# A top-k that strikes out the 16 lowest of 128 scores, and causal products grouped behind three tiles' products

## The chip, the core and the metric

The kernel runs on one core of one Trainium2 chip. The metric is the device time of one execution in microseconds (us). The core has five instruction queues that run side by side and meet only at semaphores: TensorE (PE, matrix products; its weight loads are listed apart as PEld), VectorE (DVE), ScalarE (ACT), GpSimd (POOL) and SyncE (SP, which issues DMAs). Products land in PSUM, where VectorE and ScalarE fetch them; everything else lies in SBUF.

## The reference

One decoder layer of 512 tokens (plus 16 meta tokens in front, 528 keys in all) with two attention branches, cut to what matters here:

```python
# branch A: an indexer scores every key, the best `topk` = 128 are attended to
rel = einsum('bqhd,bkd->bqhk', qi, ki) * scale_i
idx_score = einsum('bqhk,bqh->bqk', relu(rel), wi)
idx_score = where(s_pos < N_META, inf, idx_score)      # the 16 meta tokens are always picked
idx_score = where(causal, idx_score, -inf)
_, sel = lax.top_k(idx_score, topk)                    # so 112 of the others
valid = sel <= t_pos
la = einsum('bqhd,bqkhd->bqhk', qa, k_sel) * scale_a + bias
pa = softmax(where(valid, la, NEG))
# branch B: latent attention over all keys, 8 heads
lb = (q_nope @ k_nope + q_pe @ k_pe) * scale_b
lb = where(causal, lb, NEG)
pb = softmax(lb)
# then
mixed = concat([oa * silu(ga), ob * silu(gb)])
out = layer_norm(ALPHA * h + mixed @ w_out)
```

## The kernel before, in words

The 512 query rows are four tiles of 128 (`QT`). Tile i sees the 16 meta keys and 128(i+1) further ones, so `NK` is 144, 272, 400 and 528 columns. The indexer's scores of all tiles lie in `iw` with 128, 256, 384 and 512 columns.

**Order of the work.** `schedule()` writes one list, `ORDER`, by hand, and each engine walks it and takes its part of each entry. A projection job (`J`) is a group of products into one of two alternating banks of `ps_j`; ScalarE, VectorE or both read it out, and TensorE may start the job after the next only when this bank is free (line 1194 is the product of nearly all jobs). The jobs named below: `qn` and `kn` make queries and keys of two heads of branch B (`q_b`, `k_b`; ScalarE takes one head at lines 745 and 749, VectorE the other at lines 971 and 975), `va` makes values (`v_a`, ScalarE, line 756), `uv` the values of branch B.

**Top-k.** It needs 112 of up to 512 scores a row. One round finds the eight largest of a row (`max`, MAX8, line 1037) and overwrites them in place with `TAKEN` (`match_replace`, line 1041, with a short load of the eight values ahead). 14 rounds (`ROUNDS`) are made on each tile. Each round has two halves (`TOPK_HALF`): a long one with tile 3 (512 columns) and a short one with tiles 0, 1 and 2. `pick(n)` puts the next n half rounds into the order, 28 in all: 7 in two groups between the last projection jobs ahead of branch B, 3 ahead of its first values, the rest between the heads. Behind the last, `MASK` (line 1047) makes from `iw` a mask that is 2^100 where a score was not taken; branch A's heads need it.

**Heads.** Entries `S`, `X`, `R`, `TP` and `PV` with g = 0 to 15 are the heads: 0 to 7 of branch B, 8 to 15 of branch A. `S` is the scores in `ps_s`: TensorE, in two units, tiles 3, 1 and 0 first and then tile 2 (`UNITS`), and row minima on VectorE (`mn`, line 1069; signs are turned, so minima stand for maxima). `X` is the exponential on ScalarE (`pr`, line 835), `R` the reciprocal on VectorE (line 1083) and the scaling on GpSimd (line 648), `TP` transposes (line 1404 on), `PV` the product with the values. TensorE's `S` of a head waits until ScalarE has read the scores of the head before.

**Causal products.** For heads 0 to 7 the last 144 columns of each tile's scores get 2^100 added where a key lies in the future. It is a product too, of a bf16 identity with the bf16 table `causal` (line 1389), accumulated into the same columns behind the tile's fp32 product (line 1385; each appears as two instructions, tile 3 in two pieces of 240 and 288 columns).

Of the kernel before, what the change touches and what calls it, by code (L numbers as in the profile page):

```python
# [25 lines left out]
P = 128  # L26
# [87 lines left out]
def schedule():  # L114
# [42 lines left out]
    def pick(count):  # L157

        for _ in range(min(count, len(halves))):
            order.append(("TOPK", *halves.pop(0)))  # L160

    for h in range(HEADS):
# [11 lines left out]
        if h in (3, 4):  # L174
            order.append(("CAST", h - 3))
    job("qpe", 1)
    pick(2)
    job("gate", 6, extra=0)
    pick(5)
    job("uv", 0, 0, extra=0)  # L180
    job("uv", 0, 1, extra=0)
    need(BLOCKS[0], 2)
# [13 lines left out]
    for g in range(2 * HEADS):  # L196
        p = (g % HEADS) // 2
        more = p + 1 < PAIRS

        if g < HEADS:  # L200
            jobs = [("va", *va.pop(0)) for _ in range((1, 1, 2, 0, 2, 1, 2, 0)[g])]
            if g % 2 and more:
                jobs = [("qn", p + 1)] + jobs + [("kn", p + 1, 0), ("kn", p + 1, 1)]
            if g == HEADS - 1:
                jobs = [("qa", 0), ("ka", 0, 0), ("ka", 0, 1)]
        elif more:
            jobs = [("ka", p + 1, 0), ("ka", p + 1, 1)] if g % 2 else [("qa", p + 1)]
        else:
            jobs = [("out", *outs.pop(0)) for _ in range(6 if g % 2 == 0 else 4)]
        pair = (g - 3) // 2 if g >= 3 and g % 2 else None  # L210
        late = pair is not None and g >= HEADS - 1 and more or g == HEADS - 1
        order.append(("S", g))
        if g > HEADS and g % 2 and more:
            job(*jobs.pop(0), extra=0)
        order.append(("X", g))
        if g < HEADS:
            pick(1)
        if jobs[0][0] == "qn":
            order.append(("QPE", jobs[0][1]))
            job(*jobs.pop(0), extra=0)  # L220
            order[-2:] = order[:-3:-1]
        if pair is not None and not late:
            order += [("PV", pair, 0), ("PV", pair, 1)]
        if g >= HEADS and not more:
            for _ in range(3 if g % 2 == 0 else 2):
                job(*jobs.pop(0))
        order.append(("R", g))
        if HEADS <= g < 2 * HEADS - 2:
            order.append(("FOLD", g - HEADS + 2))
        if g < HEADS and g % 2 == 0:  # L230
            pick(1 if g == 0 else 2)
        if g == HEADS - 1:
            assert not halves
            order += [("MASK",), ("BIAS",), ("FOLD", 0), ("FOLD", 1)]
        for n, j in enumerate(jobs):
            if late and n == len(jobs) - 1:
                order.append(("PV", pair, 0))
            job(*j, extra=int(j[0] == "out"))
        if g < HEADS - 1 and g % 2:
            pick(1)  # L240
        if g:
            order += [("TP", g - 1), ("J", "tq", g - 1, 0)]
        if late:
            order.append(("PV", pair, 1))
        need(BLOCKS[0], 2)
        if HEADS + 1 <= g < HEADS + 5:
            order.append(("MIX", 4 + g - HEADS - 1))
        if g == 2 * HEADS - 2:
            order += [("MIX", 0), ("MIX", 1)]
# [36 lines left out]
MIXED = [s[1] for s in ORDER if s[0] == "MIX"]  # L286
LAST_JOB = [NJ[last_reader(_b)] for _b in range(len(BLOCKS))]
LAST_IN_JOB = max(n for n, j in enumerate(JOBS) if j[0] not in ("out", "tq"))
TOPK_HALF = [(3,), (0, 1, 2)]


def build(nc, x, meta, ln_emb_g, ln_emb_b, rel_bias, ln_post_g, ln_post_b, weights, gains, onehot, cos_t,
# [6 lines left out]
    with ctx:  # L299
# [26 lines left out]
        identb = sb("identb", [P, P], BF16)  # L326
        causal = sb("causal", [P, 144], BF16)
        wi = sb("wi", [P, QT, HEADS])
        top8 = sb("top8", [P, QT, 8])
        st = sb("st", [P, 5, 2, 6])  # L330
        st4 = sb("st4", [P, 4, 6])
# [45 lines left out]
        post_g, post_b = pr[:, 0, 0:D], pr[:, 1, 0:D]  # L377
        oh_sb = iw[0:BUCKETS, 0:VECW]
        vec_sb = mix[0:HEADS, 0:2, :].rearrange("p a n -> p (a n)")[:, 0:VECW]

        ps_s = ctx.enter_context(nc.psum_tensor("ps_s", [P, 1536], F32))
        ps_t = ctx.enter_context(nc.psum_tensor("ps_t", [P, 1024], F32))
# [68 lines left out]
        bn_s = sem("bn_s")  # L451
        eps = sem("eps")
        kp = sem("kp")
        squared = sem("squared")
        rope_m = sem("rope_m")

# [409 lines left out]
        def _(dve):  # L866
# [51 lines left out]
            for stage, *arg in ORDER:  # L918
# [76 lines left out]
                elif stage == "SWAP":  # L995
                    dve.wait_ge(job_act, BY_ACT[NJ["kk", 0, 1] + 1])
                    dve.stream_shuffle(k_b[HD:HD + ROPE, 0, :], k_b[HD:HD + ROPE, 1, :], SWAP).then_inc(kp, 1)
                elif stage == "NORM":
                    n = arg[0]
                    dve.wait_ge(root, (6, 8)[n])  # L1000
# [27 lines left out]
                elif stage == "TOPK":  # L1028

                    r, half = arg  # L1030
                    tiles, done = TOPK_HALF[half], topk[half]
                    if r == 0:
                        dve.wait_ge(i_add, 4 * HEADS)
                    for n, i in enumerate(tiles):
                        if r:
                            dve.wait_ge(done, len(tiles) * (2 * r - 1) + n + 1)
                        dve.max(top8[:, i, :], iw[:, IOFF[i]:IOFF[i] + P * (i + 1)]).then_inc(done, 1)  # L1037
                    for n, i in enumerate(tiles):
                        a = iw[:, IOFF[i]:IOFF[i] + P * (i + 1)]
                        dve.wait_ge(done, len(tiles) * 2 * r + n + 1)  # L1040
                        dve.match_replace(out=a, in_to_replace=top8[:, i, :], in_values=a,  # L1041
                                          imm_value=TAKEN).then_inc(done, 1)
                elif stage == "MASK":
                    for half in range(2):
                        dve.wait_ge(topk[half], 2 * len(TOPK_HALF[half]) * ROUNDS)
                    for i in range(QT):
                        dve.tensor_scalar(mask[:, POFF[i] + META:POFF[i] + NK[i]],
                                          iw[:, IOFF[i]:IOFF[i] + P * (i + 1)], TAKEN, MASKED, ALU.is_gt,
                                          ALU.mult).then_inc(masked, 1)
                    dve.wait_ge(masked, QT)  # L1050

                    dve.tensor_tensor(mask[:, 0:144], mask[:, 0:144], causal[:, :], ALU.add).then_inc(masked, 1)
# [104 lines left out]
        def _(pe):  # L1157
# [59 lines left out]
            for stage, *arg in ORDER:  # L1217
# [140 lines left out]
                elif stage == "S":  # L1358
# [14 lines left out]
                    for u, tiles in enumerate(UNITS):  # L1373
# [6 lines left out]
                        for i in tiles:  # L1380
                            for a, b in ([(0, 240), (240, 528)] if i == 3 else [(0, NK[i])]):
                                dst = ps_s[:, SOFF[i] + a:SOFF[i] + b]
                                if g < HEADS:
                                    c0 = NK[i] - 144
                                    pe.matmul(dst, q_b[:, e, i * P:(i + 1) * P], k_b[:, e, a:b], start=True,  # L1385
                                              stop=b <= c0)
                                    if b > c0:
                                        lo = max(a, c0)
                                        last = pe.matmul(ps_s[:, SOFF[i] + lo:SOFF[i] + b], identb[:, :],
                                                         causal[:, lo - c0:b - c0], start=False, stop=True)  # L1390
                                else:
                                    for v in range(2):
                                        last = pe.matmul(dst, qs[:, p % 2, e, i * P:(i + 1) * P], ks[:, e, v, a:b],  # L1393
                                                         start=v == 0, stop=v == 1)
                        last.then_inc(s_mm, 1)
                elif stage == "TP":

# [113 lines left out]
```

## Time and profile before

| | |
|---|---|
| median of three runs | 356.42 us (355.7 to 357.35) |
| the profiled execution | 356.88 us, span of its instructions 355.1 us |
| TensorE busy, mean granted clock | 329.3 us (93%), 0.992 |
| VectorE busy | 233.6 us (66%) |
| ScalarE busy | 171.5 us (48%) |
| GpSimd busy | 188.0 us (53%) |

A span is the time from the first instruction to the last. The profile's views used below: a page with shares and groups; the chain of work that ended last, followed back from the last instruction; a list of who waited for whom; groups of instructions by shape; and a timeline, where neighbours of one kind are merged and the time idle ahead of them stands in brackets. Records of one engine may overlap by the part of an instruction that is pipelined, so the chain's pieces, which don't overlap, give what each adds.

### The profile page before, as it was taken

The page shows a single profiled execution, that of the slowest core. Times are in us where ns is not written, and L with a number is a line of the kernel's source. Part 1 is how long each engine was busy: PE and PEld are TensorE (multiplying, and loading weights), DVE is VectorE, ACT ScalarE, POOL GpSimd, SP SyncE. Part 2 cuts the span into 40 slices and gives each one's busy share as a digit, 9 for nine tenths or more (in the row PEclk, how much of TensorE's full clock was granted, in tenths as well). Part 3 has the DMA queues.
Part 4 walks back from the last instruction along what each step waited for, and adds up shares of the span by engine and source line. Part 5 has one row for each costly group of instructions (what it writes and reads, how often), then busy time and mean ns, then how long its engine had stood idle before and what let it go on. Part 6 is the DMA issues. An engine that isn't in the chain of part 4 may idle for free.

```text
span 355.1 us, 6148 instructions
## 1 busy us (share of the span) xinstructions
PE 329.3 (93%) x2147; PEld 272.4 (77%) x2147; DVE 233.6 (66%) x618; ACT 171.5 (48%) x378; POOL 188.0 (53%) x172
## 2 busy tenths in 40 slices
PE   1799999999999979999999999999898999999991
PEld 1488887878778758886878887887776897897980
DVE  6762210289865999897985875557787866434666
ACT  4674543352463435556543553763775653612230
POOL 4432999777240442455313495876765581640564
PEclk9999999999999999999999999999999999999996
DMA  7463333249311131112200150431212110140023
GB/s 278 154 212 142 122 116 115 90 122 304 116 59 59 61 119 34 57 59 71 68 7 9 59 210 3 137 101 50 81 56 90 60 53 10 59 121 0 2 118 118
DMA packets 11565, 32.86 MB, mean 93 GB/s; under 512 B 2392, under 2 KB 2392, under 8 KB 11536
## 3 DMA queue, kind: packets, MB, share of 16 engines
q1 hardware_dynamic: 8944, 27.08, 22.4%
q10 hardware_dynamic: 2592, 5.40, 5.1%
q8 instruction: 17, 0.28, 0.3%
q14 instruction: 12, 0.10, 0.1%
HBM read 29.83 MB, written 4.81 MB: 98 GB/s over the span
## 4 chain that ended last, share of the span: by engine, by line
PE 72%; DVE 14%; issue 6%; ACT 6%; DMA 2%; SPq 0%; DVEq 0%; ACTq 0%
PE ps_j L1194 46%; PE ps_s L1385 5%; PE ps_o L1434 5%; PE ps_j L1236 2%; DVE iw L1041 2%; PE ps_t L1404 2%; ACT pr L835 2%; DMA res<-in_x 2%; PE ps_s L1355 2%; DVE top L1037 2%; DVE iw L1025 1%; PE ps_t L1409 1%; PE ps_s L1393 1%; DVE pr L1071 1%; PE ps_j L1247 1%
## 5 line engine op out<-in xcount | busy, mean ns | idle before, releaser
L518 POOL TENSOR_TENSOR wl<-raw,wh 128x1024 fp32r<-128x1024 f32 (+2 forms) x33 | 77.3, 2350 | 73.7 <-ACT wh L525 73.6
L1194 PE MATMUL ps_j<-hh,wh 128*128 128x512 f32 (+2 forms) x224 | 79.3, 354 | 2.4 <-DVE qs L950 1.4
L1194 PE MATMUL ps_j<-hl,wh 128*128 128x512 f32 (+2 forms) x224 | 77.9, 348 | 0.0
L1194 PE MATMUL ps_j<-hh,wl 128*128 128x512 f32 (+2 forms) x224 | 77.6, 347 | 0.0
L648 POOL TENSOR_SCALAR pr<-pr,rden 128x528 f32<-128x528 f32 (+1 forms) x64 | 34.2, 553 | 45.2 <-DVE rden L1083 45.2
L1194 PEld LDWEIGHTS ps_j<-hh,wh 128*128 128x128 f32 (+1 forms) x224 | 41.8, 186 | 13.1 <-issue 7.3
L1194 PEld LDWEIGHTS ps_j<-hh,wl 128*128 128x128 f32 (+1 forms) x224 | 41.8, 187 | 5.5
L1194 PEld LDWEIGHTS ps_j<-hl,wh 128*128 128x128 f32 (+1 forms) x224 | 41.8, 186 | 5.5 <-issue 0.2
L525 ACT ACTIVATE wh<-raw 128x1024 fp32r<-128x1024 f32 (+2 forms) x35 | 35.9, 1040 | 2.7 <-DMA raw<-in_weights 2.7
L1194 PE MATMUL ps_j<-wh,hh 128*128 128x256 f32 (+1 forms) x112 | 32.1, 287 | 1.0 <-DVE res L994 1.0
L1194 PE MATMUL ps_j<-wl,hh 128*128 128x256 f32 (+1 forms) x112 | 31.4, 281 | 0.0
L1194 PE MATMUL ps_j<-wh,hl 128*128 128x256 f32 (+1 forms) x112 | 31.4, 280 | 0.0
L658 POOL TENSOR_TENSOR bm<-bias,mask 128x144 f32<-128x144 f32 (+3 forms) x32 | 27.4, 888 | 0.0
L1041 DVE MATCH_REPLACE8 iw<-top,iw 128x512 f32<-128x512 f32 (+3 forms) x56 | 26.2, 475 | 0.0
L1037 DVE MAX8 top<-iw 128x8 f32<-128x512 f32 (+3 forms) x56 | 24.5, 478 | 0.0
L835 ACT ACTIVATE pr<-pr,mn 128x528 f32<-128x528 f32 (+3 forms) x32 | 18.0, 566 | 13.2 <-DVE mn L1071 13.1
L835 ACT ACTIVATE pr<-ps_s,mn 128x528 f32<-128x528 f32 (+3 forms) x32 | 16.9, 540 | 15.0 <-DVE mn L1069 15.0
L1385 PE MATMUL ps_s<-k_b,q_b 96*128 96x240 f32 (+4 forms) x80 | 22.3, 406 | 0.0
L1194 PEld LDWEIGHTS ps_j<-wh,hh 128*128 128x128 f32 (+1 forms) x112 | 19.6, 175 | 3.3 <-issue 2.9
L738 ACT ACTIVATE mix<-ps_j 128x512 f32<-128x512 f32 x8 | 4.8, 598 | 33.7 <-PE ps_j L1194 33.7
L1194 PEld LDWEIGHTS ps_j<-wh,hl 128*128 128x128 f32 (+1 forms) x112 | 19.6, 175 | 0.4
L1194 PEld LDWEIGHTS ps_j<-wl,hh 128*128 128x128 f32 (+1 forms) x112 | 19.6, 175 | 0.3
(224 smaller groups left out, 754.7 us busy)
## 6 DMA issues: line engine op xcount, KB each, us to landing
raw<-in_weights SPq DMA_DIRECT2D x37, 512.0 KB, 3.5
bias_by_distance<-bias_vector ACTq DMA_DIRECT2D x1, 2624.0 KB, 13.8
bias<-bias_by_distance ACTq DMA_DIRECT2D x8, 264.0 KB, 3.7
res<-in_x SPq DMA_DIRECT2D x4, 512.0 KB, 4.9
out<-res SPq DMA_DIRECT2D x3, 512.0 KB, 2.6
pt<-in_ln_emb_g SPq DMA_DIRECT2D x1, 512.0 KB, 5.5
pt<-in_ln_emb_b SPq DMA_DIRECT2D x1, 512.0 KB, 6.9
q_b<-qpe ACTq DMA_DIRECT2D x8, 64.0 KB, 2.0
```

The source lines that it names most:

```text
L518: eng.tensor_tensor(ring_of(False, b), raw_of(b), ring_of(True, b).bitcast(F32), ALU.subtract).then_inc(done, 1)
L525: act.activation(ring_of(True, b), raw_of(b), ACT.Copy).then_inc(w_high, 1)
L648: pool.tensor_scalar(a, a, rden[:, k, n:n + 1], 1.0, ALU.mult, ALU.mult).then_inc(scaled, 1)
L658: pool.tensor_tensor(bm[:, h % 2, s], bias[:, h % 4, T - NK[i]:T], mask[:, s], ALU.add).then_inc(folded, 1)
L835: act.activation(dst, src, ACT.Exp, bias=mn[:, k, n:n + 1], scale=-1.0, accum_out=den[:, k, n:n + 1]).then_inc(e_done, 1)
L1037: dve.max(top8[:, i, :], iw[:, IOFF[i]:IOFF[i] + P * (i + 1)]).then_inc(done, 1)
L1041: dve.match_replace(out=a, in_to_replace=top8[:, i, :], in_values=a, imm_value=TAKEN).then_inc(done, 1)
L1194: last = pe.matmul(dst, a, b, start=n == 0 and part[0], stop=n == count - 1 and part[1])
L1236: last = pe.transpose(bank[:, i * P:(i + 1) * P], pr[:, n % 2, a:a + P], ident[:, :])
L1355: last = pe.matmul(ibank(e, u)[:, a:a + w], qs[r, (h // 2) % 2, q, i * P:(i + 1) * P], ki[r, k, META:META + w], start=n == 0, stop=n == 2)
L1385: pe.matmul(dst, q_b[:, e, i * P:(i + 1) * P], k_b[:, e, a:b], start=True, stop=b <= c0)
L1434: last = pe.matmul(ps_o[HD * e:HD * e + HD, q0:NQ], v[0:r, j, c:c + HD], pt[0:r, e, CO[j]:CO[j] + NQ - q0], start=j == 0, stop=j == 4)
```

## The change

Two things are changed, and `pick` counts with them.

*Tile 0's top-k.* Of its 128 scores 112 are to be taken, so 16 are left. A new entry `FLIP` copies the 128 columns of tile 0 times -1 into a new tile `drop`, in reversed order of columns (`drop_back` is `drop` read or written backwards). Two rounds of MAX8 and match-and-replace on `drop` (`DROP_ROUNDS` = (128 - 112) / 8 = 2) mark the 16 lowest. The short half has three tiles in rounds 0 and 1 and two tiles, 1 and 2, in rounds 2 to 13. `MASK` reads tile 0's part from `drop_back` with the comparison the other way round. `topk_count` replaces the products that counted signals.

*Picks.* The second of the two groups ahead of branch B has 4 halves where it had 5; behind head 0 there are 2 where there was 1.

*Causal products.* They no longer stand behind each tile's product but in a loop behind the products of all tiles of the unit: three in succession in the first unit, one in the second. Tile 3's is one product of 144 columns, as before. The products of tiles 1 and 0 no longer start an accumulation of their own (`start=i >= 2`); tile 3's products, ahead of them in the same banks, do.

```diff
     job("qpe", 1)
+    order.append(("FLIP",))
     pick(2)
     job("gate", 6, extra=0)
-    pick(5)
+    pick(4)
...
         if g < HEADS and g % 2 == 0:
-            pick(1 if g == 0 else 2)
+            pick(2)
...
-TOPK_HALF = [(3,), (0, 1, 2)]
+DROP_ROUNDS = (P - PICKED) // 8
+TOPK_HALF = [lambda r: (3,), lambda r: (0, 1, 2) if r < DROP_ROUNDS else (1, 2)]
+
+
+def topk_count(r, half):
+
+    return 2 * sum(len(TOPK_HALF[half](n)) for n in range(r))
...
+        drop = sb("drop", [P, P])
...
+        drop_back = bass.AP(drop[:, :].tensor, drop[:, :].offset + P - 1, [drop[:, :].ap[0], [-1, P]])
...
+                elif stage == "FLIP":
+                    dve.wait_ge(i_add, 4 * HEADS)
+                    dve.tensor_scalar(drop_back, iw[:, IOFF[0]:IOFF[0] + P], -1.0, None, ALU.mult).then_inc(flipped, 1)
...
                     r, half = arg
-                    tiles, done = TOPK_HALF[half], topk[half]
+                    tiles, done = TOPK_HALF[half](r), topk[half]
                     if r == 0:
                         dve.wait_ge(i_add, 4 * HEADS)
+                        dve.wait_ge(flipped, 1)
                     for n, i in enumerate(tiles):
+                        a = iw[:, IOFF[i]:IOFF[i] + P * (i + 1)] if i else drop[:, :]
...
-                                          iw[:, IOFF[i]:IOFF[i] + P * (i + 1)], TAKEN, MASKED, ALU.is_gt,
-                                          ALU.mult).then_inc(masked, 1)
+                                          iw[:, IOFF[i]:IOFF[i] + P * (i + 1)] if i else drop_back, TAKEN, MASKED,
+                                          ALU.is_gt if i else ALU.is_le, ALU.mult).then_inc(masked, 1)
...
                                 if g < HEADS:
-                                    c0 = NK[i] - 144
-                                    pe.matmul(dst, q_b[:, e, i * P:(i + 1) * P], k_b[:, e, a:b], start=True,
-                                              stop=b <= c0)
-                                    if b > c0:
-                                        lo = max(a, c0)
-                                        last = pe.matmul(ps_s[:, SOFF[i] + lo:SOFF[i] + b], identb[:, :],
-                                                         causal[:, lo - c0:b - c0], start=False, stop=True)
+                                    pe.matmul(dst, q_b[:, e, i * P:(i + 1) * P], k_b[:, e, a:b], start=i >= 2,
+                                              stop=b <= NK[i] - 144, skip_group_check=True)
...
+                        if g < HEADS:
+                            for i in tiles:
+                                a = SOFF[i] + NK[i] - 144
+                                last = pe.matmul(ps_s[:, a:a + 144], identb[:, :], causal[:, :], start=False, stop=True,
+                                                 skip_group_check=True)
```

How the instructions stand now. First VectorE's queue ahead of its copy of the first `q_b`. Before (`top` is the eight values found, `iw` the scores; the last row belongs to the job `kn`):

```order
L1037 MAX top<-iw 128x8
L1041 MATCH_REPLACE iw<-top,iw 128x512
L1037 MAX top<-iw 128x8 x3
L1041 MATCH_REPLACE iw<-top,iw 128x128
L1041 MATCH_REPLACE iw<-top,iw 128x256
L1041 MATCH_REPLACE iw<-top,iw 128x384
L1037 MAX top<-iw 128x8
L1041 MATCH_REPLACE iw<-top,iw 128x512
L971 TENSOR_SCALAR q_b<-ps_j 64x512
L975 COPY k_b<-ps_j 64x264 x2
```

The same place in the changed kernel, whose line numbers are 11 to 17 higher:

```order
L1054 MAX top<-iw 128x8
L1058 MATCH_REPLACE iw<-top,iw 128x512
L1054 MAX top<-iw 128x8 x2
L1058 MATCH_REPLACE iw<-top,iw 128x256
L1058 MATCH_REPLACE iw<-top,iw 128x384
L982 TENSOR_SCALAR q_b<-ps_j 64x512
L986 COPY k_b<-ps_j 64x264 x2
```

The last long half has moved behind `q_b` and `k_b`, and the short half of round 2 has two tiles.

Second, VectorE between the row minima (`mn`) of head 0 and those of head 1. Before:

```order
L1069 TENSOR_REDUCE mn<-ps_s 128x1 x4
L1037 MAX top<-iw 128x8
L1041 MATCH_REPLACE iw<-top,iw 128x512
L1083 RECIPROCAL rden<-den 128x3
L1083 RECIPROCAL rden<-den 128x1
L1037 MAX top<-iw 128x8 x3
L1041 MATCH_REPLACE iw<-top,iw 128x128
L1041 MATCH_REPLACE iw<-top,iw 128x256
L1041 MATCH_REPLACE iw<-top,iw 128x384
L1069 TENSOR_REDUCE mn<-ps_s 128x1 x4
```

Changed:

```order
L1086 TENSOR_REDUCE mn<-ps_s 128x1 x4
L1054 MAX top<-iw 128x8 x2
L1058 MATCH_REPLACE iw<-top,iw 128x256
L1058 MATCH_REPLACE iw<-top,iw 128x384
L1100 RECIPROCAL rden<-den 128x3
L1100 RECIPROCAL rden<-den 128x1
L1054 MAX top<-iw 128x8
L1058 MATCH_REPLACE iw<-top,iw 128x512
L1054 MAX top<-iw 128x8 x2
L1058 MATCH_REPLACE iw<-top,iw 128x256
L1058 MATCH_REPLACE iw<-top,iw 128x384
L1086 TENSOR_REDUCE mn<-ps_s 128x1 x4
```

Two halves, one long and one short, have become three: short, long, short.

Third, TensorE in the scores of one head of branch B (`k_b` with `q_b` is a tile's product, `causal` with `identb` the causal one). Before:

```order
L1385 MATMUL ps_s<-k_b,q_b 128x240
L1385 MATMUL ps_s<-k_b,q_b 128x288
L1389 MATMUL ps_s<-causal,identb 128x144
L1385 MATMUL ps_s<-k_b,q_b 128x272
L1389 MATMUL ps_s<-causal,identb 128x144
L1385 MATMUL ps_s<-k_b,q_b 128x144
L1389 MATMUL ps_s<-causal,identb 128x144
L1385 MATMUL ps_s<-k_b,q_b 128x400
L1389 MATMUL ps_s<-causal,identb 128x144
```

Changed:

```order
L1401 MATMUL ps_s<-k_b,q_b 128x240
L1401 MATMUL ps_s<-k_b,q_b 128x288
L1401 MATMUL ps_s<-k_b,q_b 128x272
L1401 MATMUL ps_s<-k_b,q_b 128x144
L1410 MATMUL ps_s<-causal,identb 128x144 x3
L1401 MATMUL ps_s<-k_b,q_b 128x400
L1410 MATMUL ps_s<-causal,identb 128x144
```

The number of products is the same; the causal ones of tiles 3, 1 and 0 now follow one another.

## Rows read from the trace of the kernel before

**Rows 1.** The page, part 1: busy us, share of the span, instructions of each engine

```profile
PE 329.3 (93%) x2147; PEld 272.4 (77%) x2147; DVE 233.6 (66%) x618; ACT 171.5 (48%) x378; POOL 188.0 (53%) x172
```

**Rows 2.** The page, part 4: the chain that ended last, shares by engine

```profile
PE 72%; DVE 14%; issue 6%; ACT 6%; DMA 2%; SPq 0%; DVEq 0%; ACTq 0%
```

**Rows 3.** TensorE's waits between 105 and 206 us: us in total, times, longest

```profile
PE ps_j L1194 <- DVE q_b L971: 1.6, 1, 1.6
PE ps_j L1194 <- ACT v_a L756: 0.6, 2, 0.3
```

**Rows 4.** The chain in order of time, 119 to 136 us: start, us, what

```profile
120.59 0.97 DVE top L1037 x3
121.57 1.19 DVE iw L1041 x3
...
131.28 0.70 DVE q_b L971
...
132.12 4.35 PE ps_j L1194 x30
```

**Rows 5.** Timeline at the wait, VectorE then ScalarE: start, us, instruction [idle before]

```profile
129.78 0.68 DVE L1037 MAX8 top<-iw 128x8 f32<-128x512 f32 x1
...
130.18 0.59 ACT L745 ACTIVATE q_b<-ps_j 64x512 f32<-64x512 f32 x1 [0.80 <-PE ps_j L1194]
```

**Rows 6.** VectorE: two match loads in the timeline, then groups: busy us, mean ns

```profile
121.50 0.07 DVE L1041 MATCH_VALUE_LOAD iw<-top,iw 128x8 f32 x1
...
121.75 0.08 DVE L1041 MATCH_VALUE_LOAD iw<-top,iw 128x8 f32 x1
...
L1037 DVE MAX8 top<-iw 128x8 f32<-128x128 f32 x14 | 3.9, 281 | 0.0
...
L897 DVE TENSOR_TENSOR iw<-iw,gain 128x128 f32<-128x128 f32 x1 | 0.3, 293 | 0.0
...
L1001 DVE RECIPROCAL tmp<-tmp 128x528 f32<-128x528 f32 x1 | 3.4, 3436 | 0.0
```

**Rows 7.** The chain, transposes and scores of head 2: start, us, what

```profile
150.43 0.44 PE ps_t L1404 x4
...
151.89 0.89 PE ps_s L1385 x4
152.78 0.06 PE ps_s L1389
152.84 0.51 PE ps_s L1385 x2
...
153.41 0.29 PE ps_s L1385 x2
...
153.77 0.72 PE ps_s L1385 x2
```

**Rows 8.** TensorE's loads by shape, and line 1389's products (ns min/median/max)

```profile
L1194 PEld LDWEIGHTS ps_j<-wh,hh 128*128 128x128 f32 x96 | 18.1, 188 | 3.0 <-issue 2.9
...
L1389 PEld LDWEIGHTS ps_s<-causal,identb 128*128 128x128 bf16 x32 | 3.1, 98 | 1.9
...
L1194 PEld LDWEIGHTS ps_j<-wh,hh 128*16 128x16 f32 x16 | 1.5, 94 | 0.3
...
L1389 PE MATMUL ps_s<-causal,identb x32: 227/228/228, 137.3 to 205.3; 128*128 128x144 bf16 x32
```

**Rows 9.** Timeline of heads 0 and 1, VectorE then ScalarE

```profile
138.93 1.75 DVE L1069 TENSOR_REDUCE mn<-ps_s 128x1 f32<-128x528 f32 x4
...
144.70 1.74 DVE L1069 TENSOR_REDUCE mn<-ps_s 128x1 f32<-128x528 f32 x4
...
148.07 0.59 ACT L745 ACTIVATE q_b<-ps_j 64x512 f32<-64x512 f32 x1
...
149.18 0.38 ACT L756 ACTIVATE v_a<-ps_j 128x256 f32<-128x256 f32 x1 [0.52 <-PE ps_j L1194]
```

**Rows 10.** The chain behind head 9

```profile
242.66 0.94 ACT wh L525
```

More of the change, by code:

```diff
@@ L453, in build @@
         kp = sem("kp")
+        flipped = sem("flipped")
         squared = sem("squared")
@@ L1030, in _ @@
                     r, half = arg
-                    tiles, done = TOPK_HALF[half], topk[half]
+                    tiles, done = TOPK_HALF[half](r), topk[half]
                     if r == 0:
                         dve.wait_ge(i_add, 4 * HEADS)
+                        dve.wait_ge(flipped, 1)
                     for n, i in enumerate(tiles):
+                        a = iw[:, IOFF[i]:IOFF[i] + P * (i + 1)] if i else drop[:, :]
                         if r:
-                            dve.wait_ge(done, len(tiles) * (2 * r - 1) + n + 1)
-                        dve.max(top8[:, i, :], iw[:, IOFF[i]:IOFF[i] + P * (i + 1)]).then_inc(done, 1)
+                            last = TOPK_HALF[half](r - 1)
+                            dve.wait_ge(done, topk_count(r, half) - len(last) + last.index(i) + 1)
+                        dve.max(top8[:, i, :], a).then_inc(done, 1)
                     for n, i in enumerate(tiles):
-                        a = iw[:, IOFF[i]:IOFF[i] + P * (i + 1)]
-                        dve.wait_ge(done, len(tiles) * 2 * r + n + 1)
+                        a = iw[:, IOFF[i]:IOFF[i] + P * (i + 1)] if i else drop[:, :]
+                        dve.wait_ge(done, topk_count(r, half) + n + 1)
                         dve.match_replace(out=a, in_to_replace=top8[:, i, :], in_values=a,
@@ L1044, in _ @@
                     for half in range(2):
-                        dve.wait_ge(topk[half], 2 * len(TOPK_HALF[half]) * ROUNDS)
+                        dve.wait_ge(topk[half], topk_count(ROUNDS, half))
                     for i in range(QT):
                         dve.tensor_scalar(mask[:, POFF[i] + META:POFF[i] + NK[i]],
-                                          iw[:, IOFF[i]:IOFF[i] + P * (i + 1)], TAKEN, MASKED, ALU.is_gt,
-                                          ALU.mult).then_inc(masked, 1)
+                                          iw[:, IOFF[i]:IOFF[i] + P * (i + 1)] if i else drop_back, TAKEN, MASKED,
+                                          ALU.is_gt if i else ALU.is_le, ALU.mult).then_inc(masked, 1)
                     dve.wait_ge(masked, QT)
```

## The prediction, made before the changed kernel was run

> **What bounds the kernel now.** I read the busy shares first: TensorE is busy for 93% of the span, VectorE for 66% [rows 1]. Busy shares do not say who waits, so I went to the chain of work that ended last: 72% of it is TensorE, 14% VectorE [rows 2]. A VectorE saving is therefore worth only what it takes out of that 14%. Third, I asked for TensorE's own waits. Between 105 and 206 us one stands out, 1.6 us on a VectorE copy out of PSUM, `q_b`; behind it come two waits on ScalarE's `v_a`, 0.6 us together [rows 3]. The chain shows what stands ahead of that copy: from 119 to 131 us it runs through nothing but top-k rounds, `top` and `iw` on VectorE, then `q_b`, and then TensorE starts again at 132.12 [rows 4]. TensorE's queue is not short of work there; VectorE's queue is long. Everywhere else in the first eight heads TensorE has to be made shorter itself, or nothing is gained.
>
> **Part 1, VectorE: the tile of 128 rows leaves twelve rounds, and one half round moves behind `q_b`.** A short half round (three tiles) costs 0.97 us of MAX8 and 1.19 us of match-and-replace, 2.16 together [rows 4]. The 128-wide tile's share: its MAX8 is recorded with 281 ns [rows 6], but records of neighbours overlap. The three operations take 0.97 us for 768 columns; by columns alone 128 of them are 0.16, and I take 0.19. Its match load starts at 121.50 and the next tile's at 121.75, so 0.25 [rows 6]. Together 0.44 us a round, 12 rounds, 5.3 us less on VectorE. Only the part ahead of `q_b` can reach TensorE: one of the three short halves there loses its tile, -0.44. The moved long half takes from 129.78 to 131.28, -1.50 [rows 5]. Added is the reversed negated copy (`FLIP`). No row has an operand that runs backwards. The nearest ordinary operation of 128x128 f32 took 0.29 us [rows 6]; the slowest rate per element on this engine, the reciprocal of 528 columns in 3.44 us, would make it 0.83 [rows 6]. I take 0.3, since it is a plain multiply. VectorE would then be ready for `q_b` at 131.28 - 1.50 - 0.44 + 0.3 = 129.6 us (130.2 at the upper bound).
>
> But the data is not there at 129.6. ScalarE reads the same PSUM bank for its half of the product, waited 0.80 us for TensorE, and started at 130.18 [rows 5]. So VectorE's copy starts at 130.18 instead of 131.28, and TensorE resumes at 131.0 instead of 132.12: **1.1 us gained**. The price of `FLIP` is hidden in the 0.6 us in which VectorE now waits; only beyond that does it count. What is late next at this place is TensorE's own previous product, and the 0.5 to 0.8 us that remain idle are one copy and its signals.
>
> The other ten rounds save nothing by themselves. They lie beside TensorE's work, and after 133 us no wait of TensorE names VectorE until past the eighth head [rows 3].
>
> **What the second half round in head 0 costs.** Between the row minima of head 0 and of head 1 there stood one long and one short half; now there are one long and two short ones of 1.7 us. Before, the minima of head 0 began at 138.93 and of head 1 at 144.70, both directly behind a top-k, with no idle time ahead [rows 9]. After: three half rounds (1.4 + 1.7 + 1.4) from 132.0 end at 136.5, TensorE's scores are ready at about 137.3, minima end at 139.0, then 1.7 + 0.2 + 1.4 + 1.7 brings the minima of head 1 to about 144.1. That is 0.6 us earlier than before while TensorE is 1.3 us earlier. ScalarE's copy of the next `q_b` followed those minima by 3.4 us (148.07) [rows 9], so it comes at 147.5 and is read out at 148.0. TensorE, which ended the product before just ahead of 149.18, where ScalarE takes `v_a` [rows 9], wants that bank at about 147.85. It waits some 0.3 us. Half of this is swallowed by the wait on `v_a` that follows, because ScalarE's queue is then no longer ahead of its data. I charge **0.15 us lost**. From head 2 on VectorE is again ahead of TensorE.
>
> **Part 2, TensorE: 16 changes of operand type fewer.** For each of the first eight heads four causal products (bf16 identity as weights) stood each between two fp32 products. The rows of one head: 528 score columns took 0.89 us, 1.69 ns a column. By that 272, 144 and 400 columns should take 0.46, 0.24 and 0.67; they took 0.51, 0.29 and 0.72 [rows 7]. So the first fp32 product behind a causal one is about 0.048 us late, and the causal one itself takes 0.06. The load rows explain it. A load of 128x16 is recorded with 94 ns and one of 128x128 with 188, thus 0.84 ns a column on some 81 ns of fixed record; the fp32 weights need about 107 ns, and a causal product of 0.06 us hides only 0.06 of that. The bf16 identity is recorded with 98 ns, so about 17 above the fixed part [rows 8]: it fits behind 0.06 us. In the new order c, c, c, product, the first two causal products of each head are followed by a causal one. Each such place costs 0.06 instead of 0.06 to 0.07 plus 0.048: 0.053 saved, two a head, eight heads: **0.85 us gained**. Bounds: if a causal behind a causal came no faster than the transposes with a 128-column identity, 0.44 us for four or 0.11 each [rows 7], against 0.115 now, the gain would be 0.1; if nothing but streaming remained, 0.9.
>
> The measured load and streaming rows speak for 0.06. The Trainium skill ("TensorE: Matmul & The Clock Gate", section "Back-to-back issue gap") speaks against it: it says that in a stream of load-and-multiply pairs both set the spacing, and gives about 81 ns a pair at 128 columns. By that figure, an estimate from the page, a pair of 144 columns would take some 0.088 us and the term would be 0.4 in place of 0.85, the whole 355.0 us. No row of this trace has two bf16 pairs in succession, so the trace does not decide it.
>
> The products of tiles 1 and 0 no longer clear their accumulators first; nothing is issued more or less for it, I take 0. The mask of tile 0 is read backwards: it costs at most what the copy may cost, and VectorE waits for ScalarE behind it.
>
> **Sum.** 1.1 + 0.85 - 0.15 = 1.8 us. Everything later hangs on TensorE: the long stall after 241 us begins with ScalarE reading what TensorE just wrote, then `wh` at 242.66 [rows 10], the weight remainder on GpSimd, the mixture's remainder and the minima on VectorE. It moves as one piece, so I see no fixed point at which the 1.8 us is given back. The profiled execution took 356.88 us (span 355.1 and 1.8 around it), 0.46 above the median. Its sum gives 355.1; from the median of 356.42 it gives **354.6 us**.
>
> **Rivals.**
> *Identity loads not hidden.* Then the causal term is 0.1 and the total is 1.1 + 0.1 - 0.15 = 1.05: 355.4 us. For it: the transposes' 0.11 each. Against: their fp32 identity is recorded with a longer load than the bf16 one. The page's figure lies between, 355.0.
> *Given back in heads 0 and 1.* VectorE's extra half round delays head 1's exponentials, `q_b` and the product behind them by the whole 1.1 us; only the causal 0.85 would stay: 355.6 us. It would need the minima of head 1 no earlier than 144.7. My walk has them at 144.1, with 0.6 us between.
> *More than forecast.* The two `v_a` waits of 0.6 us [rows 3] shrink too, since ScalarE gets its exponentials earlier: 354.0 us. Against: they wait for TensorE's own product.
> *Slower: successive causal products wait for one another.* Three now accumulate in a row into two neighbouring banks. If each had to drain before the next, the step would be the 0.228 us that a causal product's record lasts from start to end [rows 8] rather than 0.06, a loss of 0.11 at 16 places, 1.8 us, against 1.0 gained: 357.2 us. From a step of about 0.18 us it decides the sign. Against: a causal product already follows the fp32 product whose very columns it adds to, with no gap between the pieces of the chain [rows 7].
> *The change doesn't do what it says.* The identity loads are all still issued, one with each product; if their number fell, the term would be at its upper end of 0.9.
>
> **Chances.** Forecast 0.57 (its own range 354.1 to 355.1). Loads partly or wholly exposed, 355.0 to 355.4, 0.20. Given back 0.08. More than forecast 0.09. Slower 0.06. The range of 8 in 10 goes from 353.7 to 356.0. A measurement here can tell about 0.5% from no change, that is 1.8 us, or 354.64: the forecast sits on this line. From the cases: faster by over 0.5%: half of the forecast's and all of the larger gain's, less a little, 0.46. Within 0.5%: 0.50. Slower by over 0.5%: 0.04.
>
> **What would show it.** TensorE's wait for `q_b` at 130 us falls from 1.6 to about 0.5 and it resumes near 131.0; `FLIP` is 0.3 us and VectorE idles ahead of `q_b`; VectorE is 5 us less busy; the chain has three causal products in about 0.18 us and then 0.72 for 400 columns; the head's scores take 2.55 us in place of 2.66. I am wrong if TensorE resumes after 131.5, if the three causal products take over 0.25 us, if a new wait over 0.4 us stands in head 1, or if TensorE's wait ahead of head 9 grows by what was gained.

## The result and the profile after

| | before | changed |
|---|---|---|
| median of 11 runs each, on one chip | 356.18 us (354.06 to 357.69) | 353.12 us (351.73 to 353.81) |
| ratio, 95% interval | | 0.991 (0.9886 to 0.9934) |
| second comparison, beside other kernels: median | 355.39 us (28 runs) | 353.45 us (11 runs) |
| ratio, 95% interval | | 0.9944 (0.9926 to 0.9963) |
| span of the profiled execution | 355.1 us | 350.2 us |
| VectorE busy | 233.6 us | 226.2 us |

The forecast was 354.6 us, 1.8 us or 0.5% below 356.42, with a range from 353.7 to 356.0. The first comparison gives 3.1 us, and 353.12 lies below the range; the second gives 1.9 to 2.0. The sign was right, the step that each part was said to make can be found in the trace, and what is to be explained is the rest. Part of it lies in the start: the forecast went out from 356.42, the median of three runs, and the kernel before had a median of 355.39 to 355.63 in four later comparisons (11 to 28 runs each). The changed kernel's two medians, 353.12 and 353.45, lie close together.

Of VectorE's 7.4 us, 2.4 belong to one subtraction that was held up in the first trace of before (below). The other four traces of before have VectorE busy for 230.6 to 230.8 us and the changed kernel's three for 226.2 to 226.4: the change takes 4.4 us off it, where 5 were forecast.

Where TensorE waits in the changed kernel between 105 and 206 us (as in [rows 3]: us in total, times, longest):

```profile
PE ps_j L1211 <- DVE q_b L982: 0.5, 1, 0.5
PE ps_j L1211 <- ACT q_b L756: 0.4, 1, 0.4
PE ps_j L1211 <- ACT v_a L767: 0.3, 1, 0.3
```

The wait of 1.6 us on `q_b` is 0.5 now, a new one of 0.4 stands in head 1, and one of the two waits on `v_a` is gone. VectorE at the place of [rows 5 and 6], and ScalarE's half of the same copy:

```profile
118.25 0.22 DVE L1011 TENSOR_SCALAR drop<-iw 128x128 f32<-128x128 f32 x1
...
129.31 0.69 DVE L982 TENSOR_SCALAR q_b<-ps_j 64x512 f32<-64x512 f32 x1 [0.45 <-PE ps_j L1211]
...
129.31 0.59 ACT L756 ACTIVATE q_b<-ps_j 64x512 f32<-64x512 f32 x1 [0.80 <-PE ps_j L1211]
```

The reversed copy took 0.22 us, and VectorE now sits idle for 0.45 us before `q_b` and starts in the same moment as ScalarE. (Both stand 0.87 us earlier than ScalarE's row of before for a reason outside the change: TensorE's granted clock rose at 16.7 us in this execution and at 18.7 in that one. When it rises differs from one execution to the next, whatever the kernel, and is taken out of the table below.) The scores of head 2 in the chain, against [rows 7]:

```profile
149.76 1.59 PE ps_s L1401 x8
151.35 0.19 PE ps_s L1410 x3
151.54 0.72 PE ps_s L1401 x2
152.27 0.07 PE ps_s L1410
```

Three causal products take 0.19 us, 0.062 each. The whole is 2.57 us instead of 2.66.

A table by stage shows where the spans differ. It is worked out from the starts of the same products, by their count, in every trace: from TensorE's stop at the first `q_b` to the transposes behind head 1 (A), to head 7 (B), to head 11 (C), to head 13 (D), and to the last product (E), in us:

| trace | A | B | C | D | E |
|---|---|---|---|---|---|
| before | 20.59 | 65.86 | 43.71 | 29.86 | 56.69 |
| before, second trace (again_before) | 21.92 | 65.88 | 43.80 | 27.76 | 56.52 |
| before, third trace (look_before_2) | 20.57 | 65.86 | 43.78 | 27.75 | 56.48 |
| changed | 19.34 | 65.21 | 43.71 | 27.81 | 56.66 |
| changed, second trace (again_after) | 19.33 | 65.21 | 43.71 | 27.81 | 56.53 |

A and B hold what was forecast: 1.25 and 0.65, together 1.9 us. Two further things show. Stage D of the forecast's own trace is 2.1 us longer than in the four others, and stage A of the kernel before is 1.35 us longer in one of its three.

**Stage D.** VectorE's subtraction `mbl` behind head 11 in the first trace of before, and then GpSimd there:

```profile
265.47 3.33 DVE L1108 TENSOR_TENSOR mbl<-mix,mbh 128x512 fp32r<-128x512 f32 x1 [0.74 <-ACT mbh L853]
...
262.70 3.19 POOL L658 TENSOR_TENSOR bm<-bias,mask 128x144 f32<-128x144 f32 x4
265.85 2.40 POOL L518 TENSOR_TENSOR wl<-raw,wh 128x1024 fp32r<-128x1024 f32 x1
```

And the same in the changed kernel:

```profile
262.70 0.97 DVE L1125 TENSOR_TENSOR mbl<-mix,mbh 128x512 fp32r<-128x512 f32 x1 [0.74 <-ACT mbh L864]
...
259.93 3.19 POOL L669 TENSOR_TENSOR bm<-bias,mask 128x144 f32<-128x144 f32 x4
263.08 2.85 POOL L529 TENSOR_TENSOR wl<-raw,wh 128x1024 fp32r<-128x1024 f32 x1
```

In both, `mbl` is issued 0.38 us before GpSimd ends its additions `bm`. In the first GpSimd goes on with `wl` at full speed (2.40) and VectorE stands until that is over. In the second VectorE goes first and `wl` takes 2.85. The times from `bm` to `mbl` are equal to 0.01 us (2.77) in the two traces, so it was not a shift between these two engines that set the order. What hangs on it: the row minima of head 12 come 2.4 us later, and TensorE waits 1.4 us on `qs`, a row that this trace of the changed kernel doesn't have. The Trainium skill ("SBUF — State Buffer", section "SBUF: two separate sides") says that VectorE with two SBUF inputs and GpSimd share a pair of ports by an exclusive lock, and that the loser stands for a whole instruction. The trace agrees on the price (3.33 = 0.38 + 2.40 + about 0.55, which is left for the subtraction itself). The rule gives the pair to whoever starts first; here VectorE was issued first, was blocked by `bm`, and then lost to the next GpSimd instruction once and won otherwise, which the rule doesn't settle.

**Stage A.** The second trace of before. The chain from `q_b` on, and engines by stretch (PE, PEld, DVE, ACT and POOL busy, then the granted clock):

```profile
130.34 0.70 DVE q_b L971
131.04 0.14 issue
131.18 5.87 PE ps_j L1194 x30
137.05 0.89 PE ps_s L1385 x4
```
```profile
132.70:136.20 3.50, 3.50 (x19) 3.50 (x19) 3.47 (x13) 0.39 (x1) 0.00 (x0) 0.51 0.15 37
```

The 30 products that took 4.35 us in [rows 4] took 5.87. From 132.7 to 136.2 us the granted clock was 0.51, the lower of the two levels (1.2 GHz of 2.4). What TensorE did before it: it had stood for 1.6 us on `q_b` and then worked without a pause from 131.18 on.

### The profile page after: what moved, and what is told of

Same layout as the page of the kernel before. It is cut to its first block, busy times and chain, and to the rows that moved or that the text cites. A ratio compares the mean times of both kernels' runs of the same rounds, so it can differ in the third digit from the quotient of the medians.

```text
span 350.2 us, 6115 instructions
## 1 busy us (share of the span) xinstructions
PE 327.1 (93%) x2147; PEld 272.4 (78%) x2147; DVE 226.2 (65%) x583; ACT 171.4 (49%) x378; POOL 188.5 (54%) x172
## 4 chain that ended last, share of the span: by engine, by line
PE 73%; DVE 11%; issue 6%; ACT 5%; POOL 2%; DMA 2%; SPq 0%; DVEq 0%; ACTq 0%; POOLq 0%
PE ps_j L1211 47%; PE ps_o L1451 5%; PE ps_s L1401 4%; PE ps_s L1405 2%; PE ps_j L1253 2%; POOL wl L529 2%; PE ps_t L1421 2%; PE ps_s L1372 2%; DMA res<-in_x 2%; ACT pr L846 2%; PE ps_t L1426 1%; DVE iw L1039 1%; DVE tmp L1015 1%; PE ps_j L1264 1%; DVE v_b L1015 1%
## 5 line engine op out<-in xcount | busy, mean ns | idle before, releaser
L1058 DVE MATCH_REPLACE8 iw<-top,iw 128x512 f32<-128x512 f32 (+2 forms) x42 | 22.6, 543 | 0.0
L1054 DVE MAX8 top<-iw 128x8 f32<-128x512 f32 (+2 forms) x42 | 21.8, 547 | 0.1
L1401 PE MATMUL ps_s<-k_b,q_b 96*128 96x240 f32 (+4 forms) x80 | 21.2, 396 | 0.0
```

The costliest lines, as they stand in the source:

```text
L1054: dve.max(top8[:, i, :], a).then_inc(done, 1)
```

## The experiments

Two theories of stage D were set against each other. A: the order of VectorE and GpSimd behind head 11 differs from execution to execution. B: the change decides it. A third, C, came later and is about stage A: the long wait on `q_b` itself makes the clock fall in part of the executions.

### A second trace of each kernel

No edit.

> The kernel before, unchanged, for a second profile. Theory A: the subtraction mbl on VectorE behind head 11 and the weight remainder wl on GpSimd fall due within 0.4 us of each other and either may go first, by chance. Then this trace may show that subtraction either with about 3.3 us (and TensorE's waits of 1.4 us on qs and a step of some 2.0 us behind it) or with about 1.0 us and none of these. Theory B: the kernel before always loses there, and the changed one always wins because of a shift the change makes: 3.3 us here again.

> The changed kernel, unchanged, for a second profile. Theory A: its subtraction mbl behind head 11 may come out at 1.0 us or at 3.3 us. Theory B: 1.0 us again.

Measured 355.14 and 354.06 us. Both traces have the quick order:

```profile
265.99 0.92 DVE L1108 TENSOR_TENSOR mbl<-mix,mbh 128x512 fp32r<-128x512 f32 x1 [0.80 <-ACT mbh L853]
```

Theory B falls as it stands: the kernel before has the quick order too. That the change makes the slow order rarer is not excluded (see the counts below). That the clock falls in this trace was not foreseen.

### Each part alone

```diff
 causal_only: before, and
-                                    pe.matmul(dst, ..., start=True, stop=b <= c0)
-                                    if b > c0:
-                                        ...   (causal product of the tile)
+                                    pe.matmul(dst, ..., start=i >= 2, stop=b <= NK[i] - 144, ...)
+                        if g < HEADS:
+                            for i in tiles:
+                                ...           (causal products of the unit)
 topk_only: the changed kernel with this turned back
```

> The kernel before with the grouped causal products alone. By the step between two causal products of 0.062 us and the head's scores of 2.57 us after, against 2.67 before, eight heads give 0.8 us: ratio 0.9977. Theory A (the order at the end of head 11 falls by chance): 0.8 us, and on average no more. Theory B (a shift of TensorE against GpSimd makes the later gain): up to 2.8 us if this part carries the shift, ratio 0.992.

> The changed kernel with each causal product back behind its tile's product. TensorE resumes 1.1 us earlier behind the first q_b, and of this some 0.15 to 0.2 goes again in head 1: 0.9 to 1.0 us, ratio 0.9973. Theory B, if this part carries the shift: up to 3 us, ratio 0.9915.

causal_only: 354.94 against 355.4, ratio 0.9981 (0.9969 to 0.9992). Its stage B is 65.32 against 65.86. Its trace shows the fall of the clock too (0.51 from 133.5 to 137.0 us), so its stage A of 21.74 is to be held against the 21.92 of the second trace of before: 0.18 less. topk_only: 353.89, ratio 0.9953 (0.9936 to 0.9971), its stages A and B are 19.43 and 65.86. In us that is 0.7 and 1.7. The causal part is as forecast. The other gives more than its 1.16 us of stage A; its interval (1.0 to 2.3) takes in that and what the clock adds (below). Neither carries 3 us.

### The order behind head 11, forced both ways

```diff
 before_hold6: before, GpSimd ahead of the weight remainder behind head 11
+                        if arg[0] in HOLD:
+                            pool.wait_ge(mix_l, MIXED.index(HOLD[arg[0]]) + 1)
 after_lose6 (and before_lose6): VectorE ahead of the subtraction there
+                    for b in HOLD:
+                        if HOLD[b] == c and not LOW_BY_DVE[b]:
+                            low_made(dve, b)
```

> The kernel before, in which GpSimd waits, ahead of the weight remainder that it makes behind head 11, until VectorE's subtraction mbl of the same place is done. VectorE then always goes first. Theory A and B alike: mbl there takes 1.0 us, TensorE's wait of 1.4 us on qs and the step before head 13's scores go, 2.0 us less than an execution that loses. Theory A: the kernel before loses in part of its executions only, so the median falls by 1 to 2 us and its spread narrows. If the later gain has another cause, the time is that of before.

> The changed kernel, in which VectorE waits, ahead of its subtraction mbl behind head 11, until GpSimd has made its weight remainder. GpSimd always goes first. mbl ends some 2.4 us later, the row minima of head 12 too, and TensorE waits for qs again: by the sum of part 1 and part 2 the kernel is then 1.6 to 1.9 us faster than before where before loses as well, ratio about 0.995 to 0.997, instead of 0.991. If the later gain has another cause, the ratio stays at 0.991.

> The kernel before, in which VectorE's subtraction behind head 11 always waits for GpSimd's weight remainder. Theory A (order by chance, slow order rare): 2.0 us slower than before, ratio 1.0055. If before were mostly in the slow order by itself: ratio 1.001 or less.

> The kernel before, a further trace. Theory A: subtraction behind head 11 at 0.9 to 1.0 us or at 3.3 us; the granted clock falls for 3.4 us at about 133 us in one of five executions.

| kernel | median | before beside it | ratio, 95% interval | stage D |
|---|---|---|---|---|
| before_hold6 | 355.51 | 355.47 | 1.0001 (0.9985 to 1.0016) | 27.81 |
| before_lose6 | 357.77 | 355.63 | 1.0065 (1.0039 to 1.0091) | 30.06 |
| after_lose6 | 355.53 | 355.47 | 1.0001 (0.9987 to 1.0015) | 30.07 |

The slow order costs 2.1 to 2.3 us in either kernel and eats the change's whole gain. Two expectations failed here. before_hold6 gained nothing where 1 to 2 us had been expected, and after_lose6 came out level with before where a ratio of 0.995 to 0.997 had been expected, for the same reason: the kernel before is in the quick order nearly always. Two more traces (look_before_3, look_before_4) had it too. Of all 13 traces in which the order was free, one has the slow order: the one from which the forecast was made. By kind it is one of seven with the old top-k (before five times, causal_only, picks_only) and none of six with the new, too few to tell whether the change matters for it.

### The count of half rounds

```diff
 picks_only: before, with
-    pick(5)
+    pick(4)
-            pick(1 if g == 0 else 2)
+            pick(2)
 after_oldpicks: the changed kernel, with these turned back
 after_pickmoved: the changed kernel, with
-            pick(2)
+            pick({0: 1, 4: 3}.get(g, 2))
```

> The kernel before with only the count of half rounds changed (4 in the second group ahead of branch B, 2 behind head 0); tile 0 stays in all 14 rounds and the causal products stay apart. VectorE is free for q_b at 131.28 - 1.50 = 129.8, still ahead of its data at 130.18, so TensorE gains the same 1.1 us there. But the minima of head 1 come 1.3 us later than in the changed kernel (three short halves of 2.2 instead of 1.7 us), and TensorE's wait on ScalarE's q_b in head 1 grows from 0.4 to 1.5 us or more: net about 0.1 us less, ratio 0.9997, if the tile's removal is needed for the gain. Rival: the gain of 1.0 us and more stands, ratio 0.997, and the 5.3 us of VectorE's work taken away were worth nothing.

> The changed kernel with the old count of half rounds (5 and 1). VectorE comes to q_b at 131.28 - 0.44 + 0.22 = 131.1, TensorE waits 1.4 us there instead of 0.5 and gains 0.2 us only; the wait on q_b in head 1 goes. By these terms 1.0 us against before (0.8 by the causal products, 0.2 here), ratio 0.997. Theory C (a wait of 1.4 us or more at this place lets TensorE's granted clock fall for some us in part of the executions; with the wait of 0.5 us it never fell in six traces): mean clocks of 0.987 to 0.989 appear among its runs again, as in 7 of 23 runs of before, and in none of the changed kernel.

> The changed kernel with one half round behind head 0 (as before) and three behind head 4. Head 1's minima come 1.4 us earlier, ScalarE's q_b too, and TensorE's wait of 0.4 us on it goes; the wait on v_a behind it comes back, some 0.25 us: net 0.1 to 0.2 us less, which five rounds cannot tell from nothing; the trace can. Rival: three half rounds behind head 4 delay head 5's minima until TensorE waits for exponentials: up to 1 us slower.

picks_only: 355.0 against 355.39, ratio 0.9994 (0.9973 to 1.0015). Two of its waits between 105 and 206 us:

```profile
PE ps_j L1194 <- ACT v_a L756: 1.4, 2, 1.1
PE ps_j L1194 <- DVE q_b L971: 0.5, 1, 0.5
```

The wait on `q_b` falls to 0.5 by the counts alone, without tile 0's removal, and comes back as one of 1.1 us in head 1, where 1.5 or more had been expected. (The list puts it down to `v_a`, but the product starts at 149.09 us, before `v_a` ends at 149.11; it comes 0.25 us behind the end of `q_b` in ScalarE, as it does in the changed kernel.) Stage A is 20.23, only 0.36 less than before. Taking tile 0 out of the short halves is what makes the moved half round affordable: 19.34. The rival, that the 5.3 us were worth nothing, falls by the traces (0.80 us of stage A between picks_only and topk_only); the ratio alone would leave it open.

after_oldpicks: ratio 0.9959 (0.9936 to 0.9982), stage A 20.18 and B 65.37, so 0.4 and 0.5. Its clock never fell in 12 runs, where theory C had expected it to. At one in five, 12 runs without a fall come about in 7 of 100 cases, so this speaks a little against C and doesn't decide it. after_pickmoved: 353.37 against 355.47, ratio 0.9936 (0.9917 to 0.9955), stage A 19.22. The 0.1 us shows in the trace alone; head 5 does not suffer (stage B 65.24).

### The changed kernel again, and a version that goes further

```diff
 after_hold: the changed kernel, with
+                        if arg[0] in HOLD:      # the remainders behind heads 9 and 11
+                            pool.wait_ge(mix_l, MIXED.index(HOLD[arg[0]]) + 1)
 best: after_pickmoved with the same
```

> The changed kernel once more beside the others on one chip. The first comparison gave 0.991 (0.9886 to 0.9934). Terms: 1.1 + 0.8 - 0.2 by the forecast, 0.4 for the clock (1.4 us in 7 of 23 executions of before), and up to 0.7 for the order of GpSimd and VectorE behind head 11 (2.0 us in one of three traces): 2.1 to 2.8 us, ratio 0.992 to 0.994.

> The changed kernel, in which GpSimd lets VectorE's subtraction go first behind head 9 and behind head 11. Behind head 9 GpSimd goes first in both traces, mbl takes 2.48 us, and TensorE waits 0.9 us and starts 1.1 us late. With VectorE first, mbl takes 0.6 to 0.7 us, the minima of head 10 come 1.8 us earlier, and TensorE's 1.1 us go: ratio 0.988 against 0.991. Rival: GpSimd's remainder, 1 us later, makes a later product wait and takes it back: 0.991.

> The changed kernel with the third half round behind head 4 instead of behind head 0, and GpSimd letting VectorE's subtraction go first behind heads 9 and 11. The sum of what the two traces showed apart: 1.1 us for the two subtractions, 0.1 to 0.2 for the half round: ratio 0.989 where the changed kernel has 0.993.

after_second: 353.45 against 355.39, ratio 0.9944 (0.9926 to 0.9963), 2.0 us. after_hold: 351.79 against 355.47, ratio 0.9897 (0.9876 to 0.9919). best: 351.72 against 355.39, ratio 0.9884 (0.9857 to 0.991), the fastest of all: 1.7 us below the changed kernel beside it. The subtraction behind head 9 in after_hold:

```profile
241.91 0.69 DVE L1136 TENSOR_TENSOR mbl<-mix,mbh 128x512 fp32r<-128x512 f32 x1 [1.00 <-ACT mbh L875]
```

In every trace without the hold it takes 2.48 us, because GpSimd starts half a microsecond ahead of it; in the changed kernel:

```profile
241.38 2.48 DVE L1125 TENSOR_TENSOR mbl<-mix,mbh 128x512 fp32r<-128x512 f32 x1 [1.00 <-ACT mbh L864]
...
240.91 2.40 POOL L529 TENSOR_TENSOR wl<-raw,wh 128x1024 fp32r<-128x1024 f32 x1 [0.46 <-ACT wh L536]
```

Stages C and D are 42.53 and 27.40 against 43.71 and 27.81, 1.6 us together. TensorE's wait of 0.9 us on ScalarE's `pt` behind head 9 is gone from the list, and nothing later takes the 1.6 us back.

### How often the clock falls

Each run gives the mean granted clock. In the traces, the three with a fall (again_before, look_before_4, causal_only) give 0.987, 0.987 and 0.988, and the others 0.992 to 0.996. Counting runs under 0.9895 (one run of before with 0.991 lies between and is not counted):

| kernels | wait on the first `q_b` | runs with a fall |
|---|---|---|
| before, beside all others | 1.6 us | 17 of 85 |
| causal_only, before_hold6, before_lose6, after_oldpicks | 1.5 to 1.6 us | 4 of 41 |
| the changed kernel and all others, picks_only among them | 0.5 us | 0 of 76 |

A fall costs 1.35 us (stage A: 21.92 and, in look_before_4, 21.95, against 20.59). At one in five that is 0.27 us in a mean. In all, 21 of 126 runs against none of 76.

The traces say more than the count, and they take most of the chance out of it. What differs between the executions of one kernel is when the clock first rose, and so how long after this rise TensorE stops at `q_b`:

| traces | clock rose | stop, after the rise | TensorE stands | fall |
|---|---|---|---|---|
| again_before, look_before_4, causal_only | 16.7 to 17.5 us | 112.58 to 112.62 | 1.88 to 1.90 | 3 of 3 |
| the three other traces of before, before_hold6, before_lose6 | 17.6 to 20.3 us | 111.22 to 112.32 | 1.89 to 1.90 | 0 of 5 |
| changed, after_hold, after_pickmoved | 16.7 to 17.2 us | 112.68 to 112.82 | 0.80 | 0 of 3 |
| after_oldpicks | 17.3 us | 112.73 | 1.77 | 0 of 1 |

("Stands" is from the start of the last product to the start of the next.) The fall came in those executions in which the clock had risen early, and with the short wait it did not come even there. So theory C is shown for the kernel before: the wait is needed, and it is not enough. The open end is after_oldpicks, whose wait of 1.77 us at nearly the same place did nothing. An early rise also brings TensorE to `q_b` earlier (129.3 to 130.1 us against 129.9 to 131.6). So a run of before with a fall is in the mean only 0.6 us longer than one without (17 and 68 runs), though the fall itself costs 1.35.

## Why the prediction was wrong where it was

*TensorE resumes 1.1 us earlier: right.* The gap behind the last product fell from 1.90 to 0.80 us, 1.10. `FLIP` took 0.22 (0.3 taken), and 0.45 us of slack were left (0.6 said).

*0.15 lost in head 1: right in kind, a little large.* ScalarE's `q_b` is waited for, 0.4 us (0.3 said), and one wait on `v_a` of 0.3 goes. Stage A is 1.25 shorter, of it 1.10 at `q_b` and 0.2 by two heads' causal products: 0.05 were lost.

*0.85 by 16 causal products: right.* 0.062 us a step was read (0.06 said), 0.10 us a head, 0.8 in all. So the loads were hidden, as the load rows had it. The 81 ns of the Trainium skill ("TensorE: Matmul & The Clock Gate", section "Back-to-back issue gap"), which would have made 0.4, did not hold for these groups of three products of 144 columns: 61 to 67 ns.

*Nothing is given back later: right.* C is the same to 0.1 us, D too where the order is the same, and E lies between 56.5 and 56.8 in either kernel.

*Nothing for the clock: wrong.* This is the step of the sum that failed. It prices the wait on `q_b` as 1.1 us of time and has no term for TensorE's clock behind it, without a reason. The clock falls behind this wait in 17 of 85 runs of before, at 1.35 us each, 0.27 in the mean, and the change removes it. With it the sum is 1.9 + 0.27 = 2.2 us, ratio 0.9939, inside the second interval and just above the first.

*The start of 356.42: too high.* The time was reached "from the median of 356.42", three runs. In the four later comparisons before has 355.39 to 355.63. From 355.39 the forecast's own 1.8 us lead to 353.6, and 353.45 was measured there: of the 1.15 us between 354.6 and 353.45, 1.0 is the start. In the first comparison before had 356.18, so the start explains only 0.2 of the 1.5 us by which 353.12 missed 354.6; 0.1 is the terms read a little low, 0.27 the clock, and the rest is open.

*One trace as what every execution does: unsafe, and harmless for the gain by luck.* The rows came from the one trace with the slow order behind head 11, 2.1 us longer in stage D. The prediction let this stretch move "as one piece", so the 2.1 us stood on both sides and dropped out of the difference. A sign stood in the rows: in the groups of before the subtraction `mbl` had a mean of 2.29 us and `hl`, the same operation on the same shape, 0.69; I called it "the mixture's remainder" and passed on. There lay also the 1.6 us that the hold gave.

*The reversed mask: not bounded as said.* It was to cost at most 0.83 us, as the copy. It took 0.96, against 0.44 for the forward read before. In both kernels it ends within 0.1 us of GpSimd's `wl`, so this is a wait and not the price of the order. Nothing hung on it.

*What stays open* is the rest of the first comparison, 3.1 - 2.2 = 0.9 us by the medians, at least 0.2 by its interval. The slow order in two or three of its eleven runs of before would do: before_lose6 runs from 357.3 to 358.5 us, and in the first comparison before has 357.35 and 357.69 at its upper end. But before_hold6, in which the order is held quick, has a run of 356.96 without a fall of the clock, so such runs have other causes too. One is when the clock first rises: in the traces it moved TensorE's stop at `q_b` between 129.3 and 131.6 us. No traces of those runs exist, so all this is argued, not shown. Nor is it shown what makes the order fall one way.

## What to carry to other kernels

A trace is one execution, and three runs are a poor start for a forecast of half a per cent: here the start was off by more than half of the gain. Before summing from a trace, compare operations of the same shape within it; an instruction that takes three times what its twin takes is a place where the next execution may differ. A wait of TensorE can cost more than its length, in the clock of what follows: the one of 1.6 us cost 1.35 us more in one execution of five. Work taken off an engine that isn't the bound pays only where it lets the order be changed: here 5.3 us were worth under 1.3 in the traces, and most of that only together with one half round moved.

## What the runs showed of the hardware

- VectorE with two SBUF inputs and GpSimd held each other up here, each for the other's whole instruction: the same 128x512 subtraction took 0.69 us alone, 0.91 to 1.00 behind the last 0.4 us of a GpSimd instruction, 2.48 behind one that had started 0.5 us ahead, and 3.33 behind such a rest and a whole one. A semaphore wait of GpSimd at two places, which fixed the order, took 1.6 us off TensorE's stages.
- In 21 of 126 runs with a TensorE wait of 1.5 us or more ahead of busy work the granted clock fell to its lower level, and with 0.5 us in none of 76. In the traces it stayed low for 3.4 us, and it fell only where the wait came 112.6 us after the clock's first rise (3 of 3), not at 111.2 to 112.3 (0 of 5).
- A row of bf16 products behind one another, each with its own 128x128 load, ran at 61 to 67 ns for 144 columns in threes; the first fp32 product behind them was late by 0.05 us (0.72 for 400 columns in place of 0.67), as it was behind each before.
- Writing 128x128 f32 backwards cost nothing visible: the copy took 0.22 us. What reading backwards costs can't be told, since the one such operation stood behind GpSimd.
